# RWKV stage: a group prepared in pairs of token blocks inside the turns, head norms with tokens on partitions

## The chip, the core and the metric

One core of a Trainium2 chip runs the whole program. The metric is device microseconds (us) of one execution; the median of three runs is given, and beside it the time and the span of the one execution that the profiler recorded. Engines: PE (TensorE, with its weight loads as PEld), DVE (VectorE), ACT (ScalarE), POOL (GpSimd), SP (which only issues DMAs). Each takes its instructions in order and waits for the others at semaphores.

## The reference

Two transformer blocks over 1024 tokens of width 1024, batch 1, float32. The first block has an RWKV mixer of 512 channels, 8 heads of 64, scanned forwards and backwards. What the change touches:

```python
w_log = -softplus(-(w0 + tanh(w_lo) @ w_up)) - 0.5      # for each of two directions
decay = exp(-exp(w_log))
a = sigmoid(a0 + a_lo @ a_up)
kk = heads(k * k_k)
kk = kk * rsqrt(maximum(sum(kk * kk, axis=-1), 1e-24))  # norm of a head's 64 channels, per token
k = k * (1.0 + (a - 1.0) * k_a)
b = kk * a
# scan:  sa = S @ -kk_t;  S = S * w_t + sa b_t^T + v_t k_t^T;  y_t = S @ r_t
bonus = sum(r * k * r_k, axis=-1) * v
```

## The kernel before

The stage is `rwkv_mix` (the block at L1127). Channels lie on partitions: `z` holds 16 tiles of 128 channels by 1024 tokens, among them r (0 to 3), k (4 to 7), v (8 to 11), the inner parts of the two decay loras (12) and of the rate lora (rows 0 to 63 of 13). Two *groups* of four heads (two tiles each) are worked one after the other. A group has 8 *turns*; turn j takes token block j of the forward direction and block 7 - j of the backward one together, 128 tokens each, in two chunks of 64. `t = 8 g + j` numbers the 16 turns.

A turn has five levels that build the inverse of a triangular matrix: PE product `mx` (L1512 is the helper of all small products), DVE mask (L1824), PE product `xx`, ACT copy `x` (L1380), DVE transpose (L1835). After them come two steps m = 0 and 1: right side (L1793), `u` (half copied by ACT, L1391, half by DVE, L1845), state update (L1849) and output. Between these, each engine has the *front* of turn t + 1 (scores, masks L1779, transposed keys, `nv` L1348) written into fixed places, and ACT the exponentials of turn t + 2 (L1314, L1320). GpSimd scales the keys (`factors`, `queries`, `ends`) and starts the inverse (`first_inverse`, L1470 and L1474). Where there is no next turn in the group (`ahead` is 0), these places are empty. All this order is written by hand, per engine.

Ahead of a group's turns stands its preparation, for each of its two tiles over all 1024 tokens: PE spreads the inverse norms over 128 rows (L1593) and forms three lora sums (L1601); ACT makes the rate (L1358), the factor of k (L1363) and two sigmoids (L1367); DVE makes kk (L1803), b (L1808) and two cumulated sums by scans (L1810, L1813); GpSimd the new k (L1485). The preparation of group 1 waits for the last state of group 0; after it come the first front and first exponentials with nothing beside them. At the end of a group DVE forms r * k * r_k in place (L1862) and ACT moves y to z (L1406).

At the start of the stage ACT squares k * k_k for four tiles (L1303), PE sums each head into rows 64 to 95 of PSUM (L1580), and DVE and ACT take maximum, root and reciprocal of a 32x1024 tile (L1770, L1305, L1773). The stationary of these sums, `head_rows`, comes with the DMA of the masks.

`Marks` are named semaphore counts: an engine adds one after each named step, and `by(name, t)` is the count that this step of turn t gives.

## Time and profile before

| | us |
|---|---|
| median of 3 runs | 3366.47 |
| lowest, highest | 3364.25, 3366.64 |
| profiled execution, its time | 3372.69 |
| profiled execution, its span (first to last instruction) | 3370.8 |
| RWKV stage in it, first DMA to the last copy of y | 688.3 to 1214.7 |
| busy: PE, PEld, DVE, ACT, POOL | 3012.5, 2455.8, 1636.2, 1059.5, 365.7 |

The profile is of one execution, 6.2 us above the median.
### The profile page before, as it was taken

To read this page: it belongs to the slowest core of one execution; us is meant where nothing else is said; L and a number is where in the kernel's file an instruction comes from. 1 tells how busy PE (TensorE), PEld (TensorE's weight loads), DVE (VectorE), ACT (ScalarE), POOL (GpSimd) and SP (SyncE) were. 2 spreads that over 40 slices of the span, in tenths; PEclk is the share of its full clock that TensorE was granted. 3 is DMA by queue.
4 is the path that set the end of the run, shared out by engine and by line. 5 is a ranking of instruction groups with operands and counts; after the bars stand their busy time and mean duration, and the time that the engine had idled before them with its cause. 6 is when DMAs were issued, how large, how long until landed. Compare 5 with 4: busy or idle time off the path is not lost.

```text
span 3370.8 us, 54412 instructions
## 1 busy us (share of the span) xinstructions
PE 3012.5 (89%) x23584; PEld 2455.8 (73%) x23584; DVE 1636.2 (49%) x2306; ACT 1059.5 (31%) x1496; POOL 365.7 (11%) x380
## 2 busy tenths in 40 slices
PE   6955569958868878999999999999999999999997
PEld 5834457828848846788888888778788788888886
DVE  4848868743444443653424332566544453334323
ACT  3232331122222222433323222553324433233322
POOL 1103322224424410000000000000000000000000
PEclk8975669968969978999999999999999999999998
DMA  3410004200000003222232222222222222223222
GB/s 123 144 38 0 0 6 142 95 29 4 4 2 4 4 28 106 89 93 94 94 100 88 94 97 97 97 85 94 91 97 94 88 94 94 100 95 119 100 94 81
DMA packets 71853, 252.79 MB, mean 75 GB/s; under 512 B 7377, under 2 KB 10321, under 8 KB 71377
## 3 DMA queue, kind: packets, MB, share of 16 engines
q1 hardware_dynamic: 62848, 217.01, 19.2%
q0 software_dynamic: 8784, 32.51, 2.7%
q8 instruction: 180, 2.95, 0.4%
q14 instruction: 41, 0.33, 0.0%
HBM read 245.29 MB, written 4.19 MB: 74 GB/s over the span
## 4 chain that ended last, share of the span: by engine, by line
PE 58%; DVE 2%; ACT 1%; issue 0%; DMA 0%; DVEq 0%; ACTq 0%
PE be_ps L2465 42%; PE be_ps L2486 14%; PE be_ps L2499 1%; DVE be_ring L2255 1%; PE be_ps L2207 0%; PE be_ps L2201 0%; ACT be_whi L2532 0%; DVE be_raw_r L2638 0%; DMA be_raw<-in_w_out 0%; DVE be_total L2220 0%; DVE ext_r L2265 0%; DVE big L2228 0%; ACT big L2538 0%; DVE big L2237 0%; ACT be_ring L2162 0%
## 5 line engine op out<-in xcount | busy, mean ns | idle before, releaser
L2638 DVE TENSOR_TENSOR be_raw_r<-be_raw,be_whi 128x1024 fp32r<-128x1024 f32 x361 | 442.3, 1225 | 991.6 <-ACT be_whi L2532 991.2
L2465 PE MATMUL be_ps<-ext_r,be_whi 128*128 128x512 f32 x2304 | 716.4, 392 | 15.3 <-PEq L1875 8.6
L2532 ACT CAST be_whi<-be_raw 128x1024 fp32r<-128x1024 f32 x361 | 378.9, 1049 | 866.6 <-DMA be_raw<-in_ffn_down 315.8
L2465 PE MATMUL be_ps<-big_r,be_whi 128*128 128x512 f32 x2048 | 641.8, 394 | 2.4 <-DVE big_r L2263 2.4
L2465 PEld LDWEIGHTS be_ps<-ext_r,be_whi 128*128 128x128 f32 x2304 | 433.8, 189 | 108.8 <-issue 10.2
L2465 PEld LDWEIGHTS be_ps<-big_r,be_whi 128*128 128x128 f32 x2048 | 383.2, 188 | 96.8 <-DVE big_r L2263 3.1
L2465 PE MATMUL be_ps<-ext_r,be_raw_r 128*128 128x512 f32 x1152 | 450.2, 391 | 0.0
L2465 PE MATMUL be_ps<-big_r,be_raw_r 128*128 128x512 f32 x1024 | 408.1, 398 | 0.0
L2486 PE MATMUL be_ps<-ext_r,be_whi 128*128 128x512 f32 x1152 | 354.6, 389 | 0.0
L2465 PEld LDWEIGHTS be_ps<-ext_r,be_raw_r 128*128 128x128 f32 x1152 | 217.7, 189 | 45.6
L2486 PEld LDWEIGHTS be_ps<-ext_r,be_whi 128*128 128x128 f32 x1152 | 216.2, 188 | 44.9
L2465 PEld LDWEIGHTS be_ps<-big_r,be_raw_r 128*128 128x128 f32 x1024 | 192.2, 188 | 44.9
L2486 PE MATMUL be_ps<-ext_r,be_raw_r 128*128 128x512 f32 x576 | 224.1, 389 | 0.0
L2486 PEld LDWEIGHTS be_ps<-ext_r,be_raw_r 128*128 128x128 f32 x576 | 108.1, 188 | 22.6
L864 PE MATMUL gm_ps_score<-gm_qk_l 64*128 64x128 f32 x448 | 59.6, 411 | 52.7 <-DVE gm_qk_l L989 52.6
L2443 POOL DMA_DIRECT2D out<-big x1 | 0.9, 852 | 973.5 <-DVE big L2237 973.5
L1512 PE MATMUL rw_ps<-rw_x,rw_by_beta 64*64 64x32 f32 x2560 | 96.1, 227 | 4.7 <-ACT rw_x L1380 2.8
L1512 PEld LDWEIGHTS rw_ps<-rw_x,rw_by_beta 64*64 64x64 f32 x2560 | 88.3, 143 | 11.9 <-ACT rw_x L1380 6.8
L864 PEld LDWEIGHTS gm_ps_score<-gm_qk_l 64*128 64x128 f32 x448 | 46.9, 283 | 66.4 <-DVE gm_qk_l L989 63.7
L2440 POOL DMA_DIRECT2D ext<-in_p x2 | 1.4, 712 | 831.3 <-PE be_ps L2486 831.3
L2566 ACT CAST ext_r<-be_gate 128x512 fp32r<-128x512 f32 x72 | 44.7, 621 | 143.4 <-DVE be_gate L2659 143.4
L2560 ACT ACTIVATE be_gate<-be_ps 128x512 f32<-128x512 f32 x88 | 52.6, 598 | 99.9 <-PE be_ps L2465 99.9
(340 smaller groups left out, 4272.8 us busy)
## 6 DMA issues: line engine op xcount, KB each, us to landing
be_raw<-in_ffn_gate SPq DMA_DIRECT2D x88, 512.0 KB, 3.3
be_raw<-in_ffn_up SPq DMA_DIRECT2D x88, 512.0 KB, 3.3
be_raw<-in_ffn_down SPq DMA_DIRECT2D x88, 512.0 KB, 3.3
be_raw<-in_conv_in SPq DMA_DIRECT2D x48, 512.0 KB, 3.3
gp_ada<-in_ada POOLq DMA_DIRECT2D x24, 512.0 KB, 3.5
rp_ada<-in_ada POOLq DMA_DIRECT2D x24, 512.0 KB, 4.4
be_raw<-in_w_out SPq DMA_DIRECT2D x16, 512.0 KB, 3.4
be_raw<-in_ple_gate SPq DMA_DIRECT2D x16, 512.0 KB, 3.3
```

Of the source, the lines that this page charges most:

```text
L864: mm = pe.matmul(ps_score[:, n % 2, par, i * BLK:(i + 1) * BLK], src[rows, 1, i], src[rows, 0, i], start=True, stop=True)
L1512: return pe.matmul(out, lhs, moving, start=start, stop=True, skip_group_check=True)
L2255: dve.scalar_tensor_tensor(s.ring[:, i % 2], self.h(i), self.gain(i), self.ps[:, 6] if plan.copy is None else s.kept[:, :], ALU.mult, ALU.mult
L2440: pool.dma_start(p_raw[:, :, cols(half)], a["p"][:, :, cols(half)]).then_inc(p_loaded[half], 16)
L2443: pool.dma_start(out[:, :, cols(0)], big[:, 0:KD, cols(0)]).then_inc(stored[0], 16)
L2465: mm = pe.matmul(ps[:, bank], part[:, k * P:(k + 1) * P], xs(k), start=(k == 0 and i == 0), stop=(k == KD - 1 and i == 2))
L2486: mm = pe.matmul(ps[:, m], part[:, m * P:(m + 1) * P], x, start=(j == 0 and i == 0), stop=(j == NF - 1 and i == 2))
L2499: mm = pe.matmul(ps[:, steps.bank[n, g]], part[:, at], x[:, k, cols(half)], start=(k == 0 and i == 0), stop=(k == 1 and i == 2))
L2532: act.copy(w.hi[:, n % 3], w.raw[:, n % 3]).then_inc(w.hi_ready, 1)
L2560: act.activation(s.gate[:, j % 2, 0:HALF], ps[:, steps.bank[n, 0]], ACT.Silu).then_inc(act_took, 1)
L2566: act.copy(inner(f, j)[0], s.gate[:, j % 2, 0:HALF]).then_inc(a_hi_made, 1)
L2638: dve.tensor_tensor(w.lo(n), w.raw[:, n % 3], w.hi[:, n % 3].bitcast(F32), ALU.subtract).then_inc(w.lo_ready, 1)
```

## The change

There is one run of 16 turns instead of two of 8. The preparation of a group is cut into four *pairs* of token blocks (p and 7 - p, 256 tokens, both tiles), which is what turns p and 7 - p need. Pair s = 4 g + p. `due(t)` says which pair is prepared in turn t: that of turn t + 2. So turns 0 and 1 prepare the last two pairs of group 0, turns 6 to 9 the four of group 1; the lora sums of the decay and their sigmoids are made at the end of the turn before (turns 0, 5, 6, 7 and 8). Pairs 0 and 1 stand ahead of turn 0, with the decay part of pair 2. `bonus` and `replace_k` of group 0 run inside turn 8. The lora and spreading products of a turn use the one PSUM bank LT, handed from engine to engine.

The head sums now have tokens on partitions: 8 products per tile, each with the squares of a block as the 128x128 stationary and a constant of 2 columns as the moving operand, into 128x64 in all. The constant is in the part that has been loaded since the beginning. The spreading takes one column of this, broadcast to 64, as the stationary and the identity as the moving operand.

```diff
+    out[:, CONST["eps"], HEAD_COLUMNS:HEAD_COLUMNS + 2] = p // 64 == np.arange(2)[None]
...
-        kk_scale = z[64:96, 13]
+        kk_scale = sb("kk_scale", [P, HEAD_PAIRS, NBLK, 2])
...
+        squares = [x[:, 0].rearrange("p d h q k t -> p (d h q k t)") for x in (by_beta, by_kappa)]
+        rate, k_factor = (z[:, 15, n * HALF:(n + 1) * HALF].rearrange("p (q n t) -> p q n t", q=2, n=2) for n in two)
...
+        AT_START = ((4, 5, 6), (1, 2, 0))
...
+        def pair_bank(bank, q):
+            return ps[:, bank, q * 4 * CH:(q + 1) * 4 * CH].rearrange("p (n t) -> p n t", n=2)
...
+        def in_pair(a, p):
+            return a.rearrange("p (n t) -> p n t", t=BLK)[:, p:NBLK - p:NBLK - 1 - 2 * p]
+        def due(t):
+            g, j = divmod(t + 2, n_turns)
+            return (g, j, n_pairs * g + j) if g < n_groups and j < n_pairs else None
+        def turns(turn):
+            for t in range(n_groups * n_turns):
+                turn(*divmod(t, n_turns), t, t % 2, min(2, n_groups * n_turns - 1 - t))
...
+            def sigmoid_of_sum(d, g, p, s, bank=LT):
+                act.wait_ge(*pe_pair.by(f"lora{d}", s))
+                if g:
+                    act.wait_ge(*act_exp.by("e_beta", g * n_turns - 1))
+                for q in two:
+                    ins = act.activation(in_pair(cum[:, d, q], p), pair_bank(bank, q), ACT.Sigmoid,
+                                         bias=vec(core, "w0", 2 * g + q + 4 * d))
+                ins.then_inc(*act_pair(f"sig{d}"))
+            def rates(g, s, bank=LT):
+                act.wait_ge(*pe_pair.by("lora_rate", s))
+                if s:
+                    act.wait_ge(*dve_pair.by("b", s - 1))
+                    act.wait_ge(*act_pair.by("k_factor", s - 1))
+                for q in two:
+                    ins = act.activation(rate[:, q], pair_bank(bank, q), ACT.Sigmoid, bias=vec(core, "a0", 2 * g + q))
+                ins.then_inc(*act_pair("rate"))
+                act.wait_ge(*act_pair.by("rate", s))
+                if s:
+                    act.wait_ge(*pool_pair.by("k", s - 1))
+                for q in two:
+                    i = 2 * g + q
+                    ins = act.activation(k_factor[:, q], rate[:, q], ACT.Identity, bias=ka_rest[:, i:i + 1],
+                                         scale=vec(core, "k_a", i))
+                ins.then_inc(*act_pair("k_factor"))
+            def exps(t):
+                g, j = divmod(t, n_turns)
+                if j < n_pairs:
+                    act.wait_ge(*dve_pair.by("cum1", n_pairs * g + j))
...
+            for p in two:
+                for d in two:
+                    sigmoid_of_sum(d, 0, p, p, AT_START[p][d])
+                rates(0, p, AT_START[p][2])
+            for d in two:
+                sigmoid_of_sum(d, 0, 2, 2)
+            exps(0)
...
+                    if n == 1 and due(t):
+                        rates(due(t)[0], due(t)[2])
+                    if n == 3 and ahead == 2:
+                        exps(t + 2)
...
+                if g and j == 0:
+                    replace_k(g - 1)
+                if ahead:
+                    v_out(t + 1, 1 - par)
+                for m in two:
+                    act.wait_ge(*pe_made.by(f"u{m}", t))
+                    act.copy(u[chunks[0]].rearrange("p h q t -> p (h q t)"), ps[chunks[0], R0 + 1, P:3 * P]
+                             ).then_inc(*act_made(f"u{m}"))
+                    if m == 0 and ahead:
+                        nv_out(t + 1, dve_made.by("rhs1", t))
+                    if due(t + 1):
...
+                        sigmoid_of_sum(m, *due(t + 1))
...
+            def replace_k(g):
+                act.wait_ge(y_taken, (g + 1) * n_turns)
                 act.wait_ge(*dve_group.by("rk", g))
                 for q in two:
                     act.copy(z[:, 4 + 2 * g + q], y[:, q]).then_inc(k_replaced, 1)
...
+            def new_keys(g, p, s):
+                pool.wait_ge(*act_pair.by("k_factor", s))
+                pool.wait_ge(*dve_pair.by("kk", s))
                 for q in two:
-                    k_i = z[:, 4 + 2 * g + q]
-                    pool.wait_ge(*act_pair.by("k_scale", 2 * g + q))
-                    pool.wait_ge(*dve_pair.by("kk", 2 * g + q))
-                    pool.tensor_tensor(k_i, k_i, tmp, ALU.mult).then_inc(*pool_pair("k"))
-                pool.wait_ge(*pool_pair.by("k", 2 * g + 1))
-                pool.wait_ge(*dve_pair.by("b", 2 * g + 1))
...
+                    k = in_pair(z[:, 4 + 2 * g + q], p)
+                    ins = pool.tensor_tensor(k, k, k_factor[:, q], ALU.mult)
+                ins.then_inc(*pool_pair("k"))
+            for p in two:
+                new_keys(0, p, p)
...
+                if due(t):
+                    new_keys(*due(t))
+                if ahead == 2:
+                    factors(*divmod(t + 2, n_turns), t + 2)
...
+            at = CONST["eps"] * P + HEAD_COLUMNS
+            head_columns = core.const[:, at:at + 2]
             for n in range(HEAD_PAIRS):
                 pe.wait_ge(kk_squared, n + 1)
-                for hf in two:
-                    ins = pe.matmul(ps[64:96, hf], head_rows(core, n), squares[n % 2][:, hf * HALF:(hf + 1) * HALF],
-                                    start=(n == 0), stop=(n == HEAD_PAIRS - 1))
+                for j in range(NBLK):
+                    ins = pe.matmul(ps[:, 0, (n * NBLK + j) * 2:(n * NBLK + j) * 2 + 2],
+                                    squares[n % 2][:, j * BLK:(j + 1) * BLK], head_columns, start=True, stop=True)
                 ins.then_inc(kk_summed, 1)
-            pe.wait_ge(kk_scaled, 2)
-            pe.wait_ge(setup, 2)
+            pe.wait_ge(setup, 1)
             pe.wait_ge(cleared, 2)
...
+            pe.wait_ge(loaded, 16)
+            def lora_sum(name, g, p, s, bank=LT):
+                n, rows, w_n, z_n = {"lora0": (0, slice(0, 64), 0, 12), "lora1": (1, slice(64, 128), 0, 12),
+                                     "lora_rate": (2, slice(0, 64), 1, 13)}[name]
+                pe.wait_ge(lora_loaded, g * 16 + 16)
+                if name == "lora0" and s >= 2:
+                    pe.wait_ge(*dve_pair.by("kk", s - 1))
+                elif bank == LT:
+                    pe.wait_ge(*act_pair.by({"lora1": "sig0", "lora_rate": "sig1"}[name], s))
+                for q in two:
+                    ins = pe.matmul(pair_bank(bank, q), lora[rows, w_n, q], in_pair(z[rows, z_n], p), start=True, stop=True)
+                ins.then_inc(*pe_pair(name))
+            def spread_kk_scale(g, p, s, bank=LT):
+                pe.wait_ge(kk_scaled, 3)
+                if bank == LT:
+                    pe.wait_ge(*act_pair.by("rate", s))
+                for q in two:
+                    for n, j in enumerate((p, NBLK - 1 - p)):
+                        for h in heads:
+                            of_head = kk_scale[:, 2 * g + q, j, h:h + 1].to_broadcast([P, CH])
+                            ins = pe.matmul(pair_bank(bank, q)[rows_of(h), n], of_head, cst(core, "ident"),
+                                            start=True, stop=True)
                 ins.then_inc(*pe_pair("kk_scale"))
...
+            for p in two:
+                for name, bank in zip(("lora0", "lora1", "lora_rate"), AT_START[p]):
+                    lora_sum(name, 0, p, p, bank)
+                if p:
+                    pe.wait_ge(*dve_pair.by("kk", 0))
+                spread_kk_scale(0, p, p, 7)
+            lora_sum("lora0", 0, 2, 2)
+            lora_sum("lora1", 0, 2, 2)
...
+                    if n == 1 and due(t):
+                        lora_sum("lora_rate", *due(t))
+                    if n == 2 and due(t):
+                        spread_kk_scale(*due(t))
...
+                    if due(t + 1) and m == 0:
+                        lora_sum("lora0", *due(t + 1))
+                    if m and ahead:
+                        front_nv(t + 1, 1 - par)
+                    if due(t + 1) and m:
+                        lora_sum("lora1", *due(t + 1))
...
+            per_head = kk_scale.rearrange("p n j h -> p (n j h)")
+            dve.tensor_scalar(per_head, ps[:, 0, 0:HEAD_PAIRS * NBLK * 2], 1e-24, None, ALU.max).then_inc(kk_scaled, 1)
             dve.wait_ge(setup, 2)
-            dve.reciprocal(kk_scale, kk_scale).then_inc(kk_scaled, 1)
+            dve.reciprocal(per_head, per_head).then_inc(kk_scaled, 1)
+            dve.wait_ge(kk_scaled, 2)
+            dve.tensor_scalar(per_head, per_head, -1.0, None, ALU.mult).then_inc(kk_scaled, 1)
+            def cumulated(d, g, p, s):
+                dve.wait_ge(*act_pair.by(f"sig{d}", s))
+                mask = keep[:, 0:BLK] if d == 0 else keep[:, BLK:0:-1]
+                for q in two:
+                    for j in (p, NBLK - 1 - p):
+                        x_block = cum[:, d, q, j * BLK:(j + 1) * BLK]
+                        x_block = x_block if d == 0 else x_block[:, ::-1]
+                        ins = dve.tensor_tensor_scan(x_block, mask, x_block, 0.0, ALU.mult, ALU.add)
+                ins.then_inc(*dve_pair(f"cum{d}"))
+            def removal_keys(g, p, s, bank=LT):
+                dve.wait_ge(*pe_pair.by("kk_scale", s))
+                if g:
+                    dve.wait_ge(*pool_front.by("alpha", g * n_turns - 1))
+                for q in two:
+                    i = 2 * g + q
+                    ins = dve.scalar_tensor_tensor(in_pair(kk[:, q], p), in_pair(z[:, 4 + i], p), vec(core, "k_k", i),
+                                                   pair_bank(bank, q), ALU.mult, ALU.mult)
+                ins.then_inc(*dve_pair("kk"))
+            def removals(g, p, s):
+                dve.wait_ge(*act_pair.by("rate", s))
+                dve.wait_ge(*dve_pair.by("kk", s))
+                if g:
+                    dve.wait_ge(*pool_front.by("beta", g * n_turns - 1))
+                for q in two:
+                    ins = dve.scalar_tensor_tensor(in_pair(b[:, q], p), in_pair(kk[:, q], p), -1.0, rate[:, q],
+                                                   ALU.mult, ALU.mult)
+                ins.then_inc(*dve_pair("b"))
...
+            def bonus(g):
+                dve.wait_ge(*pool_front.by("rho", (g + 1) * n_turns - 1))
...
+                    if due(t) and n in (1, 2):
+                        cumulated(n - 1, *due(t))
+                    if due(t) and n == 3:
+                        removal_keys(*due(t))
+                    if due(t) and n == 4:
+                        removals(*due(t))
+                    if g and j == 0 and n == 4:
+                        bonus(g - 1)
...
+                if j == n_turns - 1 and g + 1 < n_groups:
+                    empty_state(g + 1)
+            turns(turn)
+            bonus(n_groups - 1)
```

Three places show how the order moves. First ACT, the end of turn 6 (`rw_u` is the half of u, twice; `rw_x` begins the next turn). Before:

```order
L1341 COPY rw_v_tok<-rw_ps 128x2x4x64
L1391 COPY rw_u<-rw_ps 64x256
L1348 COPY rw_nv<-rw_ps 128x512
L1391 COPY rw_u<-rw_ps 64x256
L1380 COPY rw_x<-rw_ps 128x2x64x2
```

Of the change:

```order
L1386 COPY rw_v_tok<-rw_ps 128x2x4x64
L1426 COPY rw_u<-rw_ps 64x256
L1393 COPY rw_nv<-rw_ps 128x512
L1328 ACT_TABLE_LOAD
L1328 ACTIVATE rw_cum<-rw_ps,vec 128x2x128 x2
L1426 COPY rw_u<-rw_ps 64x256
L1328 ACTIVATE rw_cum<-rw_ps,vec 128x2x128 x2
L1411 COPY rw_x<-rw_ps 128x2x64x2
```

A table load and two sigmoids stand ahead of the second copy of u.

Then DVE, levels 1 to 4 of turn 1 (the masks of the products are `rw_mx`; `rw_by_beta` and `rw_by_kappa` are those of the front). Before:

```order
L1835 STREAM_TRANSPOSE rw_xt<-rw_x 128x512
L1824 TENSOR_TENSOR rw_mx<-rw_ps,rw_masks 128x2x32x4
L1779 TENSOR_TENSOR rw_by_beta<-rw_ps,rw_masks 128x512
L1835 STREAM_TRANSPOSE rw_xt<-rw_x 128x512
L1779 TENSOR_TENSOR rw_by_beta<-rw_ps,rw_masks 128x512
L1824 TENSOR_TENSOR rw_mx<-rw_ps,rw_masks 128x2x16x8
L1779 TENSOR_TENSOR rw_by_kappa<-rw_ps,rw_masks 128x512
L1835 STREAM_TRANSPOSE rw_xt<-rw_x 128x512
L1779 TENSOR_TENSOR rw_by_kappa<-rw_ps,rw_masks 128x512
L1824 TENSOR_TENSOR rw_mx<-rw_ps,rw_masks 128x2x8x16
```

Of the change:

```order
L1930 STREAM_TRANSPOSE rw_xt<-rw_x 128x512
L1848 SCALAR_TENSOR_TENSOR rw_cum<-rw_masks,rw_cum 128x128 x4
L1919 TENSOR_TENSOR rw_mx<-rw_ps,rw_masks 128x2x32x4
L1875 TENSOR_TENSOR rw_by_beta<-rw_ps,rw_masks 128x512
L1930 STREAM_TRANSPOSE rw_xt<-rw_x 128x512
L1875 TENSOR_TENSOR rw_by_beta<-rw_ps,rw_masks 128x512
L1848 SCALAR_TENSOR_TENSOR rw_cum<-rw_masks,rw_cum 128x128 x4
L1919 TENSOR_TENSOR rw_mx<-rw_ps,rw_masks 128x2x16x8
L1875 TENSOR_TENSOR rw_by_kappa<-rw_ps,rw_masks 128x512
L1930 STREAM_TRANSPOSE rw_xt<-rw_x 128x512
L1875 TENSOR_TENSOR rw_by_kappa<-rw_ps,rw_masks 128x512
L1857 SCALAR_TENSOR_TENSOR rw_kk<-big,vec,rw_ps 128x256 x2
```

Scans (`rw_cum`) and the removal keys (`rw_kk`) stand ahead of the masks of the following products.

Last PE, the second step of turn 7 of the kernel before, from its last products to the first of the next group:

```order
L1512 MATMUL rw_ps<-rw_u,rw_beta_tok 64x64 x8
L1512 MATMUL rw_ps<-rw_by_beta,rw_u 64x64 x8
L1593 MATMUL rw_ps<-big,rw_masks 128x512 x2
L1601 MATMUL rw_ps<-big,rw_lora 128x512 x6
L1593 MATMUL rw_ps<-big,rw_masks 128x512 x2
L1601 MATMUL rw_ps<-big,rw_lora 128x512 x6
L1512 MATMUL rw_ps<-rw_queried,rw_beta 64x128 x16
```

Of the change, the same place in turn 7, with the front of turn 8 (`rw_v_tok`) and a lora sum, and then the first product of turn 8:

```order
L1559 MATMUL rw_ps<-rw_v_tok,rw_by_kappa 64x64 x16
L1645 MATMUL rw_ps<-big,rw_lora 128x256 x2
L1559 MATMUL rw_ps<-rw_by_kappa,rw_v_tok 64x64 x8
L1559 MATMUL rw_ps<-rw_u,rw_beta_tok 64x64 x8
L1559 MATMUL rw_ps<-rw_by_beta,rw_u 64x64 x8
L1559 MATMUL rw_ps<-rw_x,rw_by_beta 64x32 x16
```

The wide products between the groups are gone, and a lora sum stands between the front and the output product.

## Rows read from the trace of the kernel before

**Rows 1.** The page, part 1: busy us, share of the span, instructions.
```profile
PE 3012.5 (89%) x23584; PEld 2455.8 (73%) x23584; DVE 1636.2 (49%) x2306; ACT 1059.5 (31%) x1496; POOL 365.7 (11%) x380
```

**Rows 2.** Table by stretches; busy PE, PEld, DVE, ACT, POOL, then PE's clock.
```profile
690.00:762.00 72.00, 36.58 (x218) 15.94 (x220) 28.59 (x16) 23.95 (x32) 24.57 (x28) 0.59 0.08 31
...
950.00:1030.00 80.00, 53.53 (x964) 39.72 (x962) 34.80 (x40) 24.08 (x43) 29.56 (x32) 0.64 0.01 2
```

**Rows 3.** Timeline, second state updates: start us, length, engine, line; brackets: idle before.
```profile
793.00 0.42 DVE L1849 TENSOR_TENSOR rw_state<-rw_ps,rw_state_kept 128x256 f32<-128x256 f32 x1 [3.06 <-PE rw_ps L1512]
...
911.55 0.42 DVE L1849 TENSOR_TENSOR rw_state<-rw_ps,rw_state_kept 128x256 f32<-128x256 f32 x1 [2.44 <-PE rw_ps L1512]
...
937.81 0.42 DVE L1849 TENSOR_TENSOR rw_state<-rw_ps,rw_state_kept 128x256 f32<-128x256 f32 x1 [1.93 <-PE rw_ps L1512]
...
1039.62 0.42 DVE L1849 TENSOR_TENSOR rw_state<-rw_ps,rw_state_kept 128x256 f32<-128x256 f32 x1 [1.94 <-PE rw_ps L1512]
```

**Rows 4.** Timeline of the stage's start.
```profile
695.40 3.62 PE L1580 MATMUL rw_ps<-rw_by_beta,rw_masks 128*32 128x512 f32 x4 [12.38 <-DMA rw_masks<-in_const]
...
707.06 6.54 DVE L1773 RECIPROCAL big<-big 32x1024 f32<-32x1024 f32 x1 [1.12 <-ACT big L1305]
...
741.37 0.70 ACT L1320 ACTIVATE rw_e_beta<-rw_cum 128x256 f32<-128x256 f32 x2
```

**Rows 5.** Timeline, PE: wide products at either clock, whole weights, half weights.
```profile
713.66 3.78 PE L1593 MATMUL rw_ps<-big,rw_masks 32*128 32x512 f32 x4 [9.05 <-DVE big L1773]
...
976.94 1.98 PE L1593 MATMUL rw_ps<-big,rw_masks 32*128 32x512 f32 x4
...
503.50 3.74 PE L1041 MATMUL gf_rs<-const,gf_root 128*128 128x128 f32 x32
...
478.74 1.13 PE L894 MATMUL gm_ps_k<-gm_v_tok,gm_k_tok 128*64 128x128 f32 x8
```

**Rows 6.** Timeline, the wide preparation: GpSimd's k beside DVE's scans.
```profile
732.99 3.38 POOL L1485 TENSOR_TENSOR big<-big,rw_by_kappa 128x1024 f32<-128x1024 f32 x1 [5.65 <-DVE rw_kk L1803]
734.10 4.43 DVE L1810 TENSOR_TENSOR_SCAN rw_cum<-rw_masks,rw_cum 128x1024 f32<-128x1024 f32 x1
...
738.45 2.26 DVE L1813 TENSOR_TENSOR_SCAN rw_cum<-rw_masks,rw_cum 128x1024 f32<-128x1024 f32 x1
...
724.99 2.35 POOL L1485 TENSOR_TENSOR big<-big,rw_by_kappa 128x1024 f32<-128x1024 f32 x1 [26.75 <-ACT rw_by_kappa L1363]
```

**Rows 7.** Timeline: a table load, and the end of a turn on ACT and PE.
```profile
721.23 1.28 ACT L1358 ACT_TABLE_LOAD   x1 [14.20 <-PE rw_ps L1601]
...
722.52 1.11 ACT L1358 ACTIVATE rw_by_beta<-rw_ps,vec 128x1024 f32<-128x1024 f32 x1
...
886.33 0.58 ACT L1348 COPY rw_nv<-rw_ps 128x512 f32<-128x512 f32 x1 [4.11 <-PE rw_ps L1512]
...
886.82 0.36 ACT L1391 COPY rw_u<-rw_ps 64x256 f32<-64x256 f32 x1
...
887.23 0.46 PE L1512 MATMUL rw_ps<-rw_u,rw_beta_tok 64*64 64x64 f32 x16 [0.71 <-ACT rw_u L1391]
```

**Rows 8.** Timeline, DVE: level 2 of turn 4, and the bonus at the seam.
```profile
871.61 0.65 DVE L1779 TENSOR_TENSOR rw_by_beta<-rw_ps,rw_masks 128x512 f32<-128x512 f32 x1
872.18 0.41 DVE L1824 TENSOR_TENSOR rw_mx<-rw_ps,rw_masks 128x256 f32<-128x256 f32 x1
...
966.37 2.48 DVE L1862 SCALAR_TENSOR_TENSOR big<-big,vec 128x1024 f32<-128x1024 f32 x2
```

**Rows 9.** Table by stretches of 4 us in turn 6 (columns as in Rows 2).
```profile
924.00:928.00 4.00, 2.98 (x119) 2.77 (x117) 1.50 (x3) 1.35 (x4) 0.00 (x0) 1.00 0.02 4
928.00:932.00 4.00, 3.34 (x87) 2.99 (x86) 1.11 (x3) 0.66 (x2) 0.00 (x0) 0.56 0.00 0
```

**Rows 10.** Timeline, PE: the same product at either clock in turn 7.
```profile
941.01 1.12 PE L1512 MATMUL rw_ps<-rw_x,rw_by_beta 64*64 64x32 f32 x32
...
948.29 1.92 PE L1512 MATMUL rw_ps<-rw_x,rw_by_beta 64*64 64x32 f32 x32 [0.47 <-ACT rw_x L1380]
```

516 lines of the change are left out of this document (219 added, 297 removed).

## The prediction

> **What bounds the kernel now.** Begin with the page: TensorE is busy for 89% of the span [rows 1], so DVE, ACT and GpSimd matter only where TensorE waits for them. The RWKV stage lies at 688 to 1214 us. The table by stretches [rows 2] says where that stage loses time. In the 72 us at its start TensorE works for 36.6 us, and in the 80 us around the seam between the groups for 53.5, at mean clocks of 0.59 and 0.64. Next the ends of the turns, which are the second state update of each (DVE, L1849) [rows 3]. From turn 0 to turn 6 six turns take 937.81 - 793.00 = 144.8 us, 24.1 each. I call this an ordinary turn. From the end of turn 6 to the end of turn 8, also two turns, it is 1039.62 - 937.81 = 101.8 us. The reader should see the seam as one number: 53.5 us more than two ordinary turns. It holds the last turn, whose TensorE has no work for a next one and falls to the low clock, and then a preparation in which everything waits. Last, the timeline inside the stage: within a turn the engines alternate, TensorE product, DVE mask, TensorE product, ACT copy, with gaps of half a microsecond. That matters most for the price of what is added: an engine that is busy for half of a turn is not free at the place where new work is put.
>
> **What the change removes.** *The seam.* Turn 7 now carries the front of turn 8, and turn 8 follows as turn 1 follows turn 0. The two turns cost 48.3 us before any added work: a gain of **53.5 us**. The bounds are narrow: without the one turn of 26.3 us the mean is (144.8 - 26.3) / 5 = 23.7, and the gain 54.4.
>
> *The start.* Before, the constants land first (TensorE waits until 695.40), then come the head sums, one reciprocal of 6.54 us on a 32x1024 tile, two serial pairs of wide operations, and the first exponentials end at 742.07 (the second e_beta of the row at 741.37, 0.70 long) [rows 4]. Now the sums wait only for the first square, at 692.0. They are 32 products of a 128x128 weight with 2 columns, 64 records. A weight of that size with 128 columns passes in 3.74 / 32 = 0.117 us at the high clock [rows 5]; at the low clock twice that. Bounds 7.5 and 15 us; I take low for the first two head pairs' share and high after it, ending at about 702. Four tiny operations on 128x64 follow (the reciprocal by the row 6.54 / 16 = 0.41 us), about 1.4 us with their waits. Then the pairs: a lora sum of a pair is two products of 256 columns, four records; four records of 512 columns take 1.98 us at the high clock and 3.78 at the low one [rows 5], so half-width ones take 0.86 or 1.7. On DVE a pair costs eight scans of 128 columns (2.26 us for 1024 columns [rows 6], so 0.28 and some start each, 0.37; 3.0 in all) and four operations of some 0.4 (256 columns take 0.42 in the state rows [rows 3]): 4.6 us. Two pairs one after the other from about 704.5 end near 714 to 715 with the waits on GpSimd; then the third pair's lora sums and sigmoids (each waits for the other, some 5 us), a table load of 1.28 and the exponentials of turn 0: they end at about 722 or 723. Gain **19 us**; at the low clock throughout (15 us for the sums, twice 0.86 for each lora sum) it is 11, at the high clock 23. From the first exponentials to the first product of turn 0 nothing changes.
>
> **What it adds.** Group 1's four pairs go into turns 6 to 9, and group 0's last two into turns 0 and 1: six turns with a *middle* part, and five turn *ends* (0, 5, 6, 7, 8) with the lora sums of the following turn's pair. Nothing of this is free merely because its engine has idle time.
>
> *An end.* ACT must copy nv, then load the sigmoid table (the turn's exponentials displaced it), then take two sigmoids of 128x256, and only then copies its half of u for step 1. Before, u follows nv at once: 886.33 and 886.82, and the product with u starts at 887.23 [rows 7]. The load is 1.28 us, the next activation starting 0.01 after it (721.23 + 1.28 and 722.52); the sigmoids about 0.9 (1.11 for 1024 columns, a fixed share remaining). So u comes 2.2 us late. But TensorE is in order: `lora1` stands ahead of its output product and waits for the first sigmoid, so 0.86 of lora sum and 0.5 of output product follow the sigmoid instead of filling the gap. From 886.9 + 0.2 (lora0 put ahead) + 1.28 + 0.9 + 0.86 + 0.5, the product with u starts at about 890.7: **3.5 us** late. The low bound is 2.2, if TensorE's part overlaps. Five ends: **17.5 us** (11 to 20).
>
> *A middle.* Level 1: lora_rate is 0.86 us of TensorE ahead of the second product; the four scans of direction 0 (1.4 us) run under it: 1.0. Level 2: the spreading products are 16 records of 64-column weights; eight such records took 1.13 us at the low clock [rows 5], which is half of the 0.23 each that whole weights take there, so 16 take about 0.94 at the high clock. The four scans of direction 1 stand between a mask of `by_beta` and the mask of the third product, and there DVE has no gap: the row at 871.61 ends when the one at 872.18 begins [rows 8]. 0.94 + 1.4, less some slack, is 2.1. Level 3: two `kk` operations in the same kind of place, 0.8 to 0.9. Level 4: two `b` operations, of which 0.5 lies in a gap: 0.2. Together 4.2. ACT's share (a second table load and 2 us of rates) fits, since it waits about 3 us between copies. To this comes GpSimd. In the wide preparation a scan took 4.43 us instead of 2.26 while GpSimd's product of `k` (3.38 instead of 2.35) ran beside it [rows 6]: they do not run together. The scans of direction 1 start in the same instant as GpSimd's two 1.3 us operations of `first_inverse`. Bounds 0 and 2.5 us; I take 0.9, since DVE is first in the queue but not in all four scans. **5.1 us** a middle, six of them: **31 us** (25 to 40).
>
> *The bonus.* `bonus(0)`, two operations, 2.48 us [rows 8], moves from the seam into level 4 of turn 8, ahead of a mask on the chain, beside GpSimd's factors: 2.5 to 5.3, taken as **4**. The copy of y into z (2 us of ACT) lies under it.
>
> *The clock.* Ordinary turns live near the edge: after 4 us with TensorE busy for 2.98 the granted clock was 0.56 in the next four [rows 9], and that turn took 26.3 us (911.55 to 937.81) [rows 3], 2.3 over an ordinary one. Every end now holds 3 us of waiting. I charge 1.5 us for each of five, **7.5** (0 to 15).
>
> The semaphores, masks and the extra sixteen or so waits are under these. DMA: the lora weights of group 1 are asked for after turn 1 and have four turns to land.
>
> The sum: 53.5 + 19 - 17.5 - 31 - 4 - 7.5 = 12.5, so **13 us** gained. The profiled execution has a span of 3370.8 and took 3372.69, 6.2 above the median of the runs, 3366.47; the gain is taken from the median: **3353 us**.
>
> **A rule against the row.** The trace shows a table load of 1.28 us and no gap behind it [rows 7]. The Trainium skill, ScalarE: Activation LUTs, section What ACT_TABLE_LOAD costs, says that a switch also pays a drain of about 1.38 us, 2.66 together. By that rule the five loads on the path would cost 6.9 us more, an estimate from that page, and the sum would be 6. The rows of this case do not bear it out, so it is a rival only.
>
> **Rivals.** *Hidden after all*: only TensorE's own records count, 1.8 a middle and 1.1 an end: 73 - 10.8 - 5.5 = 57 gained, 3310 us. For it: DVE 49%, ACT 31% busy. Against it: [rows 8], no gap at the place. Chance 0.13. *Low clock in the loaded turns*, the one that ends slower: the waits at the ends and behind the scans take TensorE down for whole turns. A product of 32 records takes 1.12 us high and 1.92 low [rows 10], ten of them 8 us a turn, and the front and state products about half as much again: 12 us a turn. Five turns less the 7.5 charged is 52 us, so 39 lost, 3405 us; it decides from two and a quarter such turns (13 gained and 7.5 charged against 2 x 12). More likely three or four of them than five: 3380 to 3400. The clock row [rows 9] speaks for it, the bigger share of lora and spreading records against it. Chance 0.18. *The lock in full*: each middle pays 2.5 instead of 0.9, 9.6 more: 3363 us. Chance 0.12. *The start gains little*: sums and loras at the low clock, 11 instead of 19: 3361 us. Chance 0.10. *Each table load waits longer on ACT than its row says*, 1.38 more at five ends, as a pipeline that must run empty first: 3360 us. Chance 0.07.
>
> **How the numbers follow.** The forecast has 0.40, its own range 3340 to 3362. The range from 3325 to 3384 takes in the three middle rivals and the near half of the slow one; outside lie most of the hidden case and the far part of the slow one, 0.2. About 0.2% (6.7 us) is what a measurement can tell from no change. Faster: 0.36 of the forecast, 0.13, and 0.13 of the 0.29 in the three rivals near 3361: 0.62. Same: the rest of these, 0.20. Slower: 0.18.
>
> **What the new profile would show.** The step from the end of turn 6 to that of turn 8 falls from 101.8 to about 72 (48, two middles, two ends, the bonus, two clock charges); if it is near 50, the work is hidden. First e_beta ends 34 us after the stage begins instead of 54. In an end, ACT shows nv, load, sigmoid, u, and TensorE's product with u starts 3.5 us later. A scan pair under `first_inverse` shows longer scans than those of direction 0. Turns 10 to 14 stay at 24 each. What would make it wrong: scans much longer than 0.37, or a clock below 0.8 through turns 6 to 9.

## The result, and the profile after the change

The changed kernel takes 3397.16 us (median of 4 runs, 3389.85 to 3403.86), the kernel before it 3365.36 us (4 runs, 3363.84 to 3366.64, three of them those of the table ahead of the prediction). The ratio is 1.0094, with a 95% interval of 1.0070 to 1.0118: **the change makes the kernel 32 us slower**. The forecast of 3353 us and its range up to 3384 both missed, and the sign was wrong. The profiled execution has a span of 3388.1 us and took 3389.85, so it is the fastest of the four. That of the kernel before took 3372.69, 6.2 above its median. The two traces are therefore only 17 us apart, where the medians are 32.

The page, part 1, as in [rows 1]:

```profile
PE 3050.3 (90%) x23792; PEld 2511.7 (74%) x23792; DVE 1644.2 (49%) x2387; ACT 1082.4 (32%) x1554; POOL 367.1 (11%) x392
```

The share of TensorE's busy time went up, from 89% to 90%. That says nothing good: a product at the low clock is busy for longer. The start times of the second state updates (DVE, now L1952) tell more. Two of the sixteen, the ends of turns 7 and 8, as in [rows 3]; the idle time in brackets, 6.55 and 7.01 us, was 1.9 to 3.1 in the rows of before:

```profile
1006.66 0.42 DVE L1952 TENSOR_TENSOR rw_state<-rw_ps,rw_state_kept 128x256 f32<-128x256 f32 x1 [6.55 <-PE rw_ps L1559]
...
1050.07 0.42 DVE L1952 TENSOR_TENSOR rw_state<-rw_ps,rw_state_kept 128x256 f32<-128x256 f32 x1 [7.01 <-PE rw_ps L1559]
```

From all of them, read in the same way, come the lengths of the turns. "Stage to end 0" runs from the first operation of the stage on DVE to the end of turn 0; a turn n runs from the end of turn n - 1 to its own. The middle parts are in turns 0, 1 and 6 to 9, the lora sums in the ends of turns 0 and 5 to 8.

| us | before | changed |
|---|---|---|
| stage to end 0 | 104.3 | 100.6 |
| turn 1 | 23.7 | 35.6 |
| turns 2, 3, 4 | 24.3, 23.6, 23.2 | 23.9, 23.5, 23.2 |
| turn 5 | 23.8 | 27.0 |
| turn 6 | 26.3 | 41.0 |
| turn 7 | 27.5 | 41.0 |
| turn 8 | 74.3 | 43.4 |
| turn 9 | 24.8 | 36.1 |
| turns 10 to 15 together | 144.7 | 144.5 |
| whole stage, to end 15 | 520.4 | 539.6 |

The seam is gone, as it should be: turns 7 and 8 took 101.8 us and take 84.4. But turns 6 and 9, which had nothing to win, and turn 1 lose 14.7, 11.3 and 11.9 us.

Where the time goes in a loaded turn stands in the table by stretches, through turn 6 (925.2 to 966.1 us) and most of turn 7 (columns: busy PE, PEld, DVE, ACT, POOL, then PE's clock, DMA share, GB/s):

```profile
936.00:940.00 4.00, 1.03 (x20) 1.04 (x22) 3.51 (x5) 0.00 (x0) 1.92 (x2) 0.74 0.02 4
940.00:944.00 4.00, 4.00 (x96) 4.00 (x95) 2.49 (x5) 3.04 (x8) 0.46 (x1) 0.50 0.00 0
...
960.00:964.00 4.00, 1.47 (x4) 1.16 (x4) 0.00 (x0) 2.60 (x5) 2.74 (x4) 0.72 0.00 0
964.00:968.00 4.00, 4.00 (x104) 3.50 (x106) 1.43 (x4) 0.84 (x2) 0.62 (x1) 0.50 0.02 4
...
976.00:980.00 4.00, 1.03 (x31) 0.77 (x30) 4.00 (x7) 0.00 (x0) 2.57 (x2) 0.86 0.00 0
980.00:1000.00 20.00, 19.84 (x423) 18.50 (x425) 7.37 (x16) 5.67 (x13) 5.74 (x9) 0.52 0.02 4
```

In 936 to 940 TensorE works for 1.03 of 4 us. From then on the granted clock is 0.50, half speed, although TensorE is busy for nearly all of the next twelve. In 960 to 964 it starves again (1.47 of 4), in 976 to 980 once more, and each time the low clock follows, for one stretch of 4 us behind the second gap and for most of the 20 us behind the third. The two places in a turn are always the same. The first is level 2, shown here in turn 0, on the timeline (start, length, engine, line; in brackets the idle time before and what ended it):

```profile
755.67 1.33 DVE L1848 TENSOR_TENSOR_SCAN rw_cum<-rw_masks,rw_cum 128x128 f32<-128x128 f32 x4
...
761.12 3.41 DVE L1848 TENSOR_TENSOR_SCAN rw_cum<-rw_masks,rw_cum 128x128 f32<-128x128 f32 x4
...
761.29 1.31 POOL L1514 TENSOR_TENSOR rw_by_beta<-rw_by_beta,rw_masks 128x512 f32<-128x512 f32 x1 [9.65 <-DVE rw_by_beta L1875]
762.67 1.26 POOL L1518 TENSOR_TENSOR rw_xt<-rw_by_beta,rw_masks 128x512 f32<-128x512 f32 x1
764.46 0.39 DVE L1919 TENSOR_TENSOR rw_mx<-rw_ps,rw_masks 128x256 f32<-128x256 f32 x1
...
764.90 1.81 PE L1559 MATMUL rw_ps<-rw_mx,rw_xt 64*64 64x32 f32 x29 [2.97 <-DVE rw_mx L1919]
```

The four scans of direction 0 take 1.33 us. The same four of direction 1 take 3.41, because GpSimd's two operations of `first_inverse` (1.31 and 1.26) lie inside them, and TensorE stands still for 2.97 us until the mask behind them is done.

The second place is the end of a turn, here turn 6 (ACT copies nv, loads a table, takes the sigmoid, copies u; TensorE's `lora1` stands ahead of the product with u):

```profile
955.47 0.42 DVE L1952 TENSOR_TENSOR rw_state<-rw_ps,rw_state_kept 128x256 f32<-128x256 f32 x1 [2.23 <-PE rw_ps L1559]
...
959.65 0.58 ACT L1393 COPY rw_nv<-rw_ps 128x512 f32<-128x512 f32 x1 [6.47 <-PE rw_ps L1559]
960.26 1.28 ACT L1328 ACT_TABLE_LOAD   x1
...
961.55 0.84 ACT L1328 ACTIVATE rw_cum<-rw_ps,vec 128x256 f32<-128x256 f32 x2
...
962.28 0.35 ACT L1426 COPY rw_u<-rw_ps 64x256 f32<-64x256 f32 x1
...
962.53 2.04 PE L1645 MATMUL rw_ps<-big,rw_lora 64*128 64x256 f32 x4 [2.92 <-ACT rw_cum L1328]
...
964.99 0.65 PE L1559 MATMUL rw_ps<-rw_u,rw_beta_tok 64*64 64x64 f32 x16
...
965.70 0.42 DVE L1952 TENSOR_TENSOR rw_state<-rw_ps,rw_state_kept 128x256 f32<-128x256 f32 x1 [6.55 <-PE rw_ps L1559]
```

TensorE waits 2.92 us for the sigmoid, then `lora1` takes 2.04 us at the low clock. From the first state update of the turn to the second, 955.47 to 965.70, it is 10.2 us, against 4.8 in an ordinary turn.

Last, the start of the stage, as in [rows 4]:

```profile
694.28 3.58 PE L1628 MATMUL rw_ps<-const,rw_by_beta 128*128 128x2 f32 x16 [9.02 <-ACT rw_by_beta L1317]
...
708.02 3.78 PE L1645 MATMUL rw_ps<-big,rw_lora 64*128 64x256 f32 x12
...
729.05 0.70 ACT L1365 ACTIVATE rw_e_beta<-rw_cum 128x256 f32<-128x256 f32 x2
...
700.00:708.00 8.00, 8.00 (x38) 8.00 (x38) 0.00 (x0) 2.43 (x2) 0.58 (x2) 0.50 0.00 0
```

The head sums run at 3.4 us for each head pair, where the forecast had the later two at the high clock (16 records of 0.117, 1.9 us), with the clock at 0.50 and TensorE busy for 8.00 of 8 us. The first e_beta ends at 729.75, which is 39.2 us after the stage's block begins at 690.5, against 53.8 before. That is 14.6 us gained instead of 19.

### The profile page after: what moved, and what is told of

Read it like the earlier page. It is cut to its first block, busy times and chain, and to the rows that moved or that the text cites. A ratio compares the mean times of both kernels' runs of the same rounds, so it can differ in the third digit from the quotient of the medians.

```text
span 3388.1 us, 55041 instructions
## 1 busy us (share of the span) xinstructions
PE 3050.3 (90%) x23792; PEld 2511.7 (74%) x23792; DVE 1644.2 (49%) x2387; ACT 1082.4 (32%) x1554; POOL 367.1 (11%) x392
## 3 DMA queue, kind: packets, MB, share of 16 engines
q8 instruction: 182, 2.98, 0.4%
## 4 chain that ended last, share of the span: by engine, by line
PE 57%; DVE 2%; ACT 1%; DMA 0%; issue 0%; DVEq 0%; ACTq 0%
PE be_ps L2566 42%; PE be_ps L2587 14%; DVE be_ring L2356 1%; PE be_ps L2600 1%; PE be_ps L2308 0%; PE be_ps L2302 0%; ACT be_whi L2633 0%; DVE be_raw_r L2739 0%; DMA be_raw<-in_w_out 0%; DMA be_raw<-in_ple_gate 0%; DVE be_total L2321 0%; DVE ext_r L2366 0%; ACT big L2639 0%; DVE big L2329 0%; DVE big L2338 0%
## 5 line engine op out<-in xcount | busy, mean ns | idle before, releaser
L2566 PEld LDWEIGHTS be_ps<-ext_r,be_whi 128*128 128x128 f32 x2304 | 432.5, 188 | 108.2 <-issue 10.2
L1559 PE MATMUL rw_ps<-rw_x,rw_by_beta 64*64 64x32 f32 x2560 | 105.3, 238 | 1.9 <-ACT rw_x L1411 1.4
L1559 PEld LDWEIGHTS rw_ps<-rw_x,rw_by_beta 64*64 64x64 f32 x2560 | 99.8, 158 | 6.8 <-ACT rw_x L1411 4.0
L1559 PE MATMUL rw_ps<-rw_mx,rw_xt 64*64 64x32 f32 x2048 | 83.4, 236 | 19.4 <-DVE rw_mx L1919 18.4
L1559 PEld LDWEIGHTS rw_ps<-rw_mx,rw_xt 64*64 64x64 f32 x2048 | 78.7, 156 | 26.1 <-DVE rw_mx L1919 26.1
```

The source lines that it names most:

```text
L1559: return pe.matmul(out, lhs, moving, start=start, stop=True, skip_group_check=True)
L2566: mm = pe.matmul(ps[:, bank], part[:, k * P:(k + 1) * P], xs(k), start=(k == 0 and i == 0), stop=(k == KD - 1 and i == 2))
```

## The experiments

The theory, called A in what follows: each stall of about 3 us takes TensorE's clock to half for up to half a turn, and that, more than the added work and the stalls themselves, is the loss. Its rival B: the stalls and the added instructions cost their own length and no more. The runs were made in three sessions, in each of which the kernel before ran too (medians of 3369.23, 3367.13 and 3363.88 us), but the changed kernel did not. So a difference from its 3397.16 can be off by some 4 us; the ratio to before, given with each run, is the safer number.

### The scans freed from GpSimd, and the ends rearranged

The first edit, on GpSimd alone:

```diff
+                if due(t):
+                    pool.wait_ge(*dve_pair.by("cum1", due(t)[2]))
                 if ahead:
                     first_inverse(t + 1, 1 - par)
```

> Only GpSimd's first_inverse of a turn with a middle waits until the scans of direction 1 are done. In the changed kernel those four scans took 3.41 us instead of 1.33, and TensorE stood still for 2.97 us. Theory A (each stall of about 3 us takes the clock to 0.50 for half a turn, and the low clock is most of the loss): scans at 1.33, a gap of about 1 us, turns 1 and 9 fall from 36 to about 29 us, turns 0, 6, 7, 8 by about 5 each, since their other stall stays; median about 3363 us (3355 to 3372). Theory B (the waits alone, clock beside the point): 2.1 us in each of six middles, 12.6 in all, 3384 us. Theory C (the lock moves to the masks of level 3): scans at 1.33 but no gain, 3397 us.

Measured: 3362.81 us (10 runs, 3355.28 to 3382.75), 0.9989 of before (0.9973 to 1.0005). Turn 1, the next level 2 of that kernel:

```profile
794.60 1.36 DVE L1850 TENSOR_TENSOR_SCAN rw_cum<-rw_masks,rw_cum 128x128 f32<-128x128 f32 x4
...
796.04 1.27 POOL L1514 TENSOR_TENSOR rw_by_beta<-rw_by_beta,rw_masks 128x512 f32<-128x512 f32 x1 [10.93 <-DVE rw_cum L1850]
796.19 0.68 DVE L1877 TENSOR_TENSOR rw_by_kappa<-rw_ps,rw_masks 128x512 f32<-128x512 f32 x1
...
796.33 1.06 PE L1561 MATMUL rw_ps<-rw_mx,rw_xt 64*64 64x32 f32 x30 [0.92 <-DVE rw_mx L1921]
```

The scans are back at 1.36 us and TensorE waits 0.92 instead of 2.97. Turn 1 falls from 35.6 to 28.1 us, turn 9 from 36.1 to 32.8, turns 6, 7 and 8 by 8.8, 4.1 and 4.5. The stall that was removed is 2.1 us long, the turns fall by up to four times that, and the whole by 34 us, where B said 12.6. Turn 9 did not come down to the 29 us that A gave it. C is out as well: the stall does not move to the masks of level 3. The row of the mask into by_kappa shows it: it has one input in PSUM and one in SBUF, runs beside GpSimd's operation, and takes 0.68 us as always.

The second edit puts ACT's first sigmoids behind both copies of u, and `lora1` with its sigmoids into level 1 of the next turn:

```diff
                     if m == 0 and ahead:
                         nv_out(t + 1, dve_made.by("rhs1", t))
-                    if due(t + 1):
-                        sigmoid_of_sum(m, *due(t + 1))
+                if due(t + 1):
+                    sigmoid_of_sum(0, *due(t + 1))
...
             def turn(g, j, t, par, ahead):
+                if t and due(t):
+                    sigmoid_of_sum(1, *due(t))
...
                         from_state(t, par, 0)
+                        if t and due(t):
+                            lora_sum("lora1", *due(t))
...
-                    if due(t + 1) and m:
-                        lora_sum("lora1", *due(t + 1))
```

> Only the ends are rearranged: ACT copies nv and both halves of u before it loads the table and takes the first sigmoids, and lora1 with its sigmoids goes into level 1 of the next turn. The products with u no longer wait for a load or a sigmoid. Theory A: the stall of about 3 us at five ends goes, turn 5 falls from 27.0 to 24, turns 6, 7, 8 from 41-43 to the 36 us of turns 1 and 9, which have no such end: about 25 us in all, 3372 us (3365 to 3378). Theory B (waits alone): 3.5 us at five ends, 17.5 in all, and lora1 costs 0.9 where it stands now: 3384 us.

Measured: 3359.37 us (10 runs, 3350.68 to 3365.41), 0.9972 of before (0.9962 to 0.9981). Turn 5, which has only an end, falls from 27.0 to 23.6, as A and B both said (3.4 us). Turns 6, 7 and 8 fall from 41.0, 41.0 and 43.4 to 33.1, 30.5 and 37.4. Both theories said too little here: the gain is 38 us in all, 13 more than A and 20 more than B expected. Perhaps a turn with one stall instead of two comes back to the high clock for longer than A assumed; in this run turns 7 and 8 together have a clock of 0.87, where the changed kernel has 0.66.

> Both edits together. Theory A: no stall of 3 us is left, the granted clock stays near 1.00 through turns 1 and 5 to 9, each turn with a middle takes 24 + 4 to 5 us instead of 36 to 43: about 70 to 75 us less than the changed kernel, 3323 us (3315 to 3335), which is more than the two edits give one by one. Theory B (waits alone): the two gains add, 12.6 + 13, 3371 us.

Measured: 3329.04 us (4 runs, 3328.01 to 3333.49), 0.9888 of before (0.9871 to 0.9904). That is inside A's range and 42 us below B's number. One part of the expectation was wrong: 68 us is about the sum of the two single gains, 34 and 38, not more. Turns 6, 7 and 9 take 28.2, 28.2 and 27.8 us. Turns 7 and 8 in the table, from the end of turn 6 to the end of turn 8, first in the changed kernel, then in this one:

```profile
966.12:1050.49 84.37, 70.56 (x1532) 63.53 (x1532) 38.57 (x74) 26.17 (x54) 27.15 (x32) 0.66 0.01 2
```

```profile
928.97:991.64 62.67, 53.96 (x1535) 46.70 (x1532) 34.02 (x74) 26.03 (x55) 26.89 (x33) 0.92 0.01 3
```

The granted clock is 0.66 against 0.92, with the same work to do (1532 and 1535 of TensorE's records). In turn 7 alone it is 1.00 in this kernel, in turn 8 it is 0.85.

### The stalls left in place, and filled

This run separates clock and waits. Nothing is rearranged; in each of the two gaps TensorE gets five products that nobody needs.

```diff
+            def filler():
+                for _ in range(5):
+                    mm(ps[:, Y0, 2 * P:4 * P], cst(core, "ident"), core.const[:, 0:2 * P], start=False)
...
                     elif ahead and n == 3:
                         front_kappa(t + 1, 1 - par, 0)
+                        if due(t):
+                            filler()
...
                     if due(t + 1) and m:
+                        filler()
                         lora_sum("lora1", *due(t + 1))
```

> The changed kernel with its waits as they are, and five products of a 128x128 weight with 256 columns (about 2.2 us of TensorE at the high clock) put into each of the two stalls of a loaded turn, into columns that nobody reads. Theory A: the clock stays up although everything waits as long as before: turns 6 to 8 fall from 41-43 to about 34, turns 1 and 9 from 36 to 31, 3359 us (3350 to 3370). Theory B: nothing is gained, 3397 us or more, up to 2 us for each filler that is longer than its gap.

Measured: 3350.9 us (4 runs, 3346.27 to 3352.2), 0.9944 of before (0.9927 to 0.996). Work was added, nothing that the chain waits for was moved, and the kernel became **46 us faster** than the changed one (50 by the two ratios to before). Level 2 of turn 7, and turns 7 and 8 in the table:

```profile
953.24 3.42 DVE L1855 TENSOR_TENSOR_SCAN rw_cum<-rw_masks,rw_cum 128x128 f32<-128x128 f32 x4
...
957.03 1.06 PE L1559 MATMUL rw_ps<-rw_mx,rw_xt 64*64 64x32 f32 x29 [0.62 <-DVE rw_mx L1926]
```

```profile
944.40:1014.84 70.44, 62.31 (x1575) 53.04 (x1573) 38.14 (x73) 26.18 (x55) 27.18 (x32) 0.95 0.01 3
```

The scans are as long as ever (3.42 us), but TensorE stands idle for only 0.62 us of the gap instead of 2.97, and its clock is 0.95 in turns 7 and 8 together, and 1.00 in turns 1, 5, 6, 7 and 9. Turns 6 and 7 take 32.3 us each instead of 41.0, turn 8 38.1 instead of 43.4, turns 1 and 9 28.8 and 28.7 instead of 35.6 and 36.1, and the stage 495.9 instead of 539.6. B is out. The run also gives the waits without the clock: turn 1, with a middle only, is 5.6 us above that kernel's ordinary 23.2; turn 5, with an end only, 3.6 above.

### One such stall, in the kernel before

The kernel before the change, with nothing of the change in it, and four extra scans of constants in turns 2 and 11:

```diff
                         if ahead and n in (2, 3):
                             front_out(t + 1, 1 - par, ("beta1", "kappa1")[n - 2])
+                        if n == 2 and t in (2, 11):
+                            for k in range(4):
+                                dve.tensor_tensor_scan(idle[:, k * BLK:(k + 1) * BLK], keep[:, 0:BLK], keep[:, 0:BLK],
+                                                       0.0, ALU.mult, ALU.add)
```

> The kernel before the change, with nothing of the change in it: in turns 2 and 11 alone DVE does four extra scans of 128 columns (of constants, into columns that nobody reads) at the place where the changed kernel has those of direction 1, behind the mask by_beta of level 2 and beside GpSimd's first_inverse. Each of the two turns had 24.3 and 24.4 us. Theory A (a stall costs its length and then the low clock): the scans take about 3.4 us, TensorE stands still about 3 us, the granted clock is at 0.50 behind it and each turn gets 6 to 10 us longer, 30 to 34 us. Theory B (only its length): 26.5 to 27.5 us. The median of the whole moves by 12 to 20 us by A, by 5 to 6 by B.

Measured: 3376.93 us (7 runs, 3367.11 to 3384.16), 1.0036 of before (1.0021 to 1.0052). Turn 2, timeline and table:

```profile
818.37 3.40 DVE L1844 TENSOR_TENSOR_SCAN big<-rw_masks 128x128 f32<-128x128 f32 x4
...
822.14 1.57 PE L1513 MATMUL rw_ps<-rw_mx,rw_xt 64*64 64x32 f32 x29 [2.97 <-DVE rw_mx L1825]
...
820.00:824.00 4.00, 1.86 (x42) 1.86 (x46) 2.68 (x5) 0.13 (x1) 1.18 (x1) 0.81 0.00 0
824.00:828.00 4.00, 4.00 (x96) 4.00 (x90) 1.71 (x3) 2.30 (x8) 2.31 (x4) 0.50 0.02 4
```

The scans and the stall repeat what the changed kernel shows (3.40 us for 3.41, and 2.97 for 2.97). Turns 2 and 11 take 28.6 and 29.8 us, where that execution's ordinary turn is 23.2: 5.4 and 6.6 us for a stall of 2.97. Against the same two turns of the kernel before (24.3 and 24.4) it is 4.3 and 5.4. So a single stall costs one and a half times to twice its length. A's lower end of 30 us was too high, B's 27.5 too low; the median moved by 13 us, which is inside A's 12 to 20. The two traces do not show it over the whole stage (520.0 us here, 520.4 before): this profiled execution is 6.5 us below its median and that of before 6.2 above, and other turns, turn 6 above all (23.6 for 26.3), are shorter here. This run is the weakest of those that speak for A; e4_filler is the strongest.

### The bonus

In the kernel with both edits turn 8 still takes 34.5 us, 6.3 more than turn 7. Its level 4 on DVE and TensorE, and the clock behind it:

```profile
976.11 2.94 DVE L1912 SCALAR_TENSOR_TENSOR big<-big,vec 128x1024 f32<-128x1024 f32 x2
978.98 0.41 DVE L1923 TENSOR_TENSOR rw_mx<-rw_ps,rw_masks 128x256 f32<-128x256 f32 x1
...
979.44 1.80 PE L1563 MATMUL rw_ps<-rw_xt,rw_mx 64*64 64x32 f32 x29 [2.97 <-DVE rw_mx L1923]
...
980.00:984.00 4.00, 3.95 (x61) 3.46 (x60) 0.86 (x3) 1.99 (x4) 1.14 (x2) 0.50 0.02 4
```

The two operations of `bonus(0)` take 2.94 us beside GpSimd, TensorE waits 2.97, and the clock is 0.50 behind it: a third stall with the same sequel. The edit:

```diff
-                    if g and j == 0 and n == 4:
-                        bonus(g - 1)
+                if j == n_turns - 1 and g + 1 < n_groups:
+                    bonus(g, 0)
                 for m in two:
...
                                     ).then_inc(*dve_made(f"u{m}"))
+                    if m == 0 and j == n_turns - 1 and g + 1 < n_groups:
+                        bonus(g, 1)
                     dve.wait_ge(*pe_made.by(f"end{m}", t))
```

> The kernel with both edits (e3_both), and the two operations of bonus(0) taken out of level 4 of turn 8 and put, one by one, into gaps of DVE at the end of turn 7 (behind the last transposed block, and behind the copy of u of step 0). In e3_both turn 8 takes 34.5 us, the other loaded turns 28.2. Theory: the bonus on the chain beside GpSimd's factors costs 6.3 us, turn 8 falls to 28 to 29, turn 7 grows by 0 to 1: 3323 to 3324 us. Rival: what is long in turn 8 is the copy of y into z on ACT and the first turn of a group as such: turn 8 stays above 33 us, 3329.

Measured: 3320.25 us (4 runs, 3315.79 to 3324.6), 0.9859 of before (0.9838 to 0.988). DVE in level 5 and the end of turn 7:

```profile
949.07 1.53 DVE L1911 SCALAR_TENSOR_TENSOR big<-big,vec 128x1024 f32<-128x1024 f32 x1
...
951.08 1.28 DVE L1911 SCALAR_TENSOR_TENSOR big<-big,vec 128x1024 f32<-128x1024 f32 x1
```

Turn 8 falls to 28.9 us. Turns 6 and 7 read 29.2 instead of 28.2 in this execution; turn 6 holds nothing of the edit, so of its growth I can say no more than that such differences of a microsecond come and go. The rival, that turn 8 is long as the first turn of a group, is out.

### Level 4 instead of level 2

This kernel has the ends of e2_ends. The scans of direction 1 go to level 4, behind the mask and ahead of a transpose that has to wait for ACT anyway, and ACT's exponentials one level later. GpSimd gets no wait.

```diff
                     elif ahead and n == 5:
                         front_x(t + 1)
+                    if due(t) and n == 4:
+                        cumulated(1, *due(t))
...
-                    if due(t) and n in (1, 2):
-                        cumulated(n - 1, *due(t))
+                    if due(t) and n == 1:
+                        cumulated(0, *due(t))
...
-                    if n == 3 and ahead == 2:
+                    if n == (4 if due(t) else 3) and ahead == 2:
                         exps(t + 2)
```

> The ends of e2_ends, and instead of letting GpSimd wait, the four scans of direction 1 stand in level 4 between a mask and the transpose that waits for ACT's copy, where DVE is idle for about 1.5 us; the exponentials go one level later. Theory (a price is set by the gap at the place, not by the length of the work): a middle costs 3.5 to 4 us instead of 4.9, turn 1 takes 26.5 to 27.2, turns 6 and 7 27 instead of 28.2: 3322 to 3325 us. Rival: the factors on GpSimd come too late for kept, or the longer chain at level 4 stalls TensorE: turns of 30 us and more, 3340 us or above.

Measured: 3343.86 us (4 runs, 3343.78 to 3344.9), 0.993 of before (0.9912 to 0.9948): the rival's number. The rival had named a stall of TensorE by the longer chain at level 4 as one of two reasons; the stall is there, but it comes through ACT. Turn 1:

```profile
797.73 1.53 POOL L1531 TENSOR_TENSOR big<-big 128x256 f32<-128x256 f32 x2 [1.74 <-DVE rw_kk L1860]
797.84 2.33 DVE L1851 TENSOR_TENSOR_SCAN rw_cum<-rw_masks,rw_cum 128x128 f32<-128x128 f32 x4
...
799.53 1.28 ACT L1360 ACT_TABLE_LOAD   x1
...
802.26 0.57 ACT L1382 COPY rw_kappa_tok<-rw_ps 128x512 f32<-128x512 f32 x1
...
802.88 0.69 PE L1562 MATMUL rw_ps<-rw_masks,big 64*64 64x64 f32 x32 [2.19 <-ACT rw_kappa_tok L1382]
```

The table load and the exponentials stand ahead of ACT's copy of kappa_tok, and TensorE's next products wait 2.19 us for that copy. The scans, now beside GpSimd's product of the new keys, take 2.33 us. Turn 1 takes 30.7 us instead of 27.8. The next run puts the exponentials behind that copy, lets the new keys wait for the scans, and moves the bonus as above.

```diff
                         kappa_out(t + 1, 1 - par)
+                    if n == 4 and due(t):
+                        exps(t + 2)
...
             def new_keys(g, p, s):
                 pool.wait_ge(*act_pair.by("k_factor", s))
+                pool.wait_ge(*dve_cum.by("cum1", s))
                 pool.wait_ge(*dve_pair.by("kk", s))
```

> In e7_gap_scans TensorE stood still for 2.2 us in front of the value transposes, until ACT's kappa_tok copy, which stood behind the table load and the exponentials, and the scans took 2.33 us beside GpSimd's product of the new keys. Here the exponentials come after the kappa_tok copy, the new keys wait for the scans, and the bonus is placed as in e6_bonus. Theory: no stall is left in a middle, the clock stays up, turn 1 takes 26 to 27.5 us (27.8 in e3_both) and the loaded turns 27 to 28.5: 3312 to 3320 us, at or below e6_bonus (3320). Rival: level 4 has no more room on DVE than level 2 (kk, mask, scans and b all stand there): turns of 29 us and more, 3325 us or above.

Measured: 3317.61 us (4 runs, 3315.73 to 3318.01), 0.9861 of before (0.9844 to 0.9877). In turn 1 the copy now comes ahead of the load, and the scans have their own length:

```profile
790.48 1.36 DVE L1854 TENSOR_TENSOR_SCAN rw_cum<-rw_masks,rw_cum 128x128 f32<-128x128 f32 x4
...
792.31 0.59 ACT L1382 COPY rw_kappa_tok<-rw_ps 128x512 f32<-128x512 f32 x1 [0.15 <-PE rw_ps L1565]
```

Turn 1 takes 27.2 us, turns 6 to 9 27.6, 28.8, 28.7 and 27.3. So the work of a middle costs 4 us in the best place that I found, and the kernel stands at 3318 to 3320 us in either form, 46 to 47 us ahead of the kernel before in the same session, and 77 to 80 ahead of the changed one. Between this one and e6_bonus the intervals do not tell.

### The clock in the head sums

The kernel with both edits, with fourteen products ahead of the head sums:

```diff
             head_columns = core.const[:, at:at + 2]
+            for _ in range(14):
+                pe.matmul(ps[:, LT, 0:2 * P], cst(core, "ident"), core.const[:, 0:2 * P], start=True, stop=True)
```

> The kernel with both edits (e3_both, 3329 us), and ahead of the head sums fourteen products of a 128x128 weight with 256 columns into a bank that is overwritten later: about 6 us at the high clock, in the 8 us in which TensorE has nothing to do at the start of the stage. In the kernels so far the sums ran at 3.4 us for each head pair with the granted clock at 0.50 although TensorE was busy all the time. Theory S1 (the clock was low only because TensorE came out of a pause): it stays at 1.00 through the sums, 1.7 us for each pair unless the squares are late, the sums end 5 to 6 us earlier: 3323 us. Theory S2 (a stream of products of 2 columns does not keep the high clock): it falls back to 0.50 within the sums, the gain is 0 to 2 us: 3328 us.

Measured: 3333.04 us (4 runs, 3329.64 to 3339.19), 0.9903 of before (0.9883 to 0.9923): nothing gained, and from the stage's first operation to the end of turn 0 it is 93.2 us instead of 88.1. TensorE at the start, and the table by stretches:

```profile
689.08 8.18 PE L1630 MATMUL rw_ps<-const 128*128 128x256 f32 x28 [5.80 <-PEq L281]
697.10 1.84 PE L1634 MATMUL rw_ps<-const,rw_by_beta 128*128 128x2 f32 x16
698.80 2.69 PE L1634 MATMUL rw_ps<-const,rw_by_kappa 128*128 128x2 f32 x16
701.35 3.55 PE L1634 MATMUL rw_ps<-const,rw_by_beta 128*128 128x2 f32 x16
...
696.00:700.00 4.00, 4.00 (x32) 3.85 (x30) 0.00 (x0) 1.02 (x1) 2.83 (x5) 0.97 0.01 4
700.00:704.00 4.00, 4.00 (x20) 4.00 (x20) 0.00 (x0) 2.56 (x3) 0.00 (x0) 0.50 0.00 0
```

The added products ran at the low clock for their first part (8.18 us in place of 6), and the sums began 8.0 us after the stage's first operation instead of 3.2. The first head pair's sums then took 1.7 us, at the high clock, as S1 says; in 700 to 704 the clock is at 0.50 again although TensorE had not paused since 689. S2's course came true, but not its number: the added products cost more than they gave. Why the clock falls in this stream, the rows do not tell.

## Why the prediction was wrong

**The sum, term by term.** In the changed kernel's own runs:

- *The seam, 53.5*: right. In e6_bonus, with the bonus off the chain, turns 7 and 8 take 58.0 us. Less two middles of 4.75 (its turns 1 and 9 take 27.8 and 28.1, over 23.2) it is 48.5, and before they took 101.8: 53.3 us.
- *The start, 19*: 14.6. The mis-sized term is above all the head sums: 13.8 us instead of 10, since the clock did not rise in them as I took it to. The bound (15 us) held it. The readings of [rows 5] came out low too: half of 1.98 is 0.99 and not 0.86, and a lora sum measures 1.10 us at the high clock (e4_filler) and 2.04 at the low one; and 1.13 / 8 is 0.14 and not half of 0.23, so 16 spreading records are 1.13 at the high clock and not 0.94 (they measure 1.09).
- *The ends, 3.5 each*: right while the clock is high (1.00 there): turn 5 of e4_filler, with an end only, is 26.8 us, 3.6 over 23.2. At the low clock an end costs 5.4 (10.2 less 4.8 from one state update to the next), and from ACT's copy of nv to the product with u it is 5.3 us in place of 0.9, 4.4 more.
- *The middles, 5.1 each*: 5.6 in e4_filler's turn 1. In it the lock (DVE and GpSimd keeping each other waiting) was under-priced: the scans of direction 1 grow by 2.1 us (3.41 for 1.33), where I took 0.9 of a range to 2.5.
- *The bonus, 4*: 6.3, above its upper bound of 5.3, since it too sets off the low clock.
- *The clock, 7.5*: **44 to 50 us**. It is the difference between the changed kernel and e4_filler, 43.7 in the stage's traces, 46 in the medians and 50 by the ratios, although the filler adds some 2.4 us of work to each gap.

With the measured sizes the sum is 53.5 + 14.6 - 5 x 3.5 - 6 x 5.6 - 6.3 - 45 = -34, and the measurement is -32. That they agree so well is in part luck: in the two traces from which most of the sizes were read, the stage is only 19 us longer. About 7 us of the difference lie in turns 1 to 6 and 9 of the kernel before, which were in all 7.3 us above seven turns of 23.2; the rest was not followed up.

**The step that failed** is the sentence "I charge 1.5 us for each of five". I had the row that priced it: in [rows 9], after one stretch with 2.98 of 4 us busy, the clock was at 0.56 in the next, and the turn was 2.3 longer (26.3 less 24.1 is rather 2.2). From that I took a price for a mild gap and put it on ends in which, by my own working, TensorE would wait 3 us. And I charged the ends alone, not the middles, although the paragraph above had just shown that a mask waits behind scans there. The working on level 2 summed up what DVE has to do and never turned the same numbers round to ask how long TensorE would have nothing. It would have: 1.4 us of scans, plus up to 2.5 of lock, is a gap of up to 3.9 us in each of six turns, and 2.97 was measured. What the runs showed in its place: the gaps behind the scans and those at the ends together cost 44 to 50 us in clock alone, not 7.5, and the turns that have only a middle pay for it too (6.8 and 7.4 us in turns 1 and 9).

**The rival that came true** is the low clock in the loaded turns. Its price of 12 us for each low turn was too high, as no turn is low all the way: the clock costs 8.7 us in turns 6 and 7, 5.3 in turn 8, 6.8 and 7.4 in turns 1 and 9, 5.4 in turn 0 (changed kernel less e4_filler). But six turns have it and not five. What I set against it, the bigger share of lora and spreading records, was wrong: in the table above TensorE is busy for 19.84 of 20 us behind the gap of 976 to 980, with such records among them, and the clock there is 0.52. The chance of 0.18 should have been the largest. Its count of turns was loose too: 13 gained and 7.5 charged are used up by 1.7 turns of 12 us, not by two and a quarter. The rival of the lock in full came true beside it (2.1 of 2.5 us). *Hidden after all* is out. *The start gains little* is half true. *Each table load waits longer* is out: the load at 960.26 takes 1.28 us and the sigmoid begins at 961.55, and the stage's other loads read the same. The Trainium skill, ScalarE: Activation LUTs, section What ACT_TABLE_LOAD costs, gives 2.66 us with a drain; by these rows there is no such drain here.

**The list of what the profile would show.** Turn 6 to turn 8: 84.4, not 72. First e_beta: 39.2 us after the stage begins, not 34. The order nv, load, sigmoid, u in an end: as said. Longer scans under `first_inverse`: as said. Turns 10 to 14: 23.2 to 23.7, as said. "A clock below 0.8 through turns 6 to 9" stood under what would make it wrong, and is what happened (0.67 in turn 6, 0.66 in turns 7 and 8, 0.67 in turn 9). So did the scans much longer than 0.37, 0.85 each in direction 1.

## What to carry to other kernels

Where a tightly wound chain feeds TensorE, ask of every piece of work that is put into it how long TensorE then has nothing to do, and not only how long the piece is: here one gap of 3 us made its turn 4 to 7 us longer, and the changed kernel's gaps cost 44 to 50 us in clock on top of their own length. Two cheap remedies worked: order the small work so that nothing on the chain stands behind it on its engine (the copies of u ahead of the table load, GpSimd behind DVE's scans), or, where a gap must stay, fill it with products whose result is thrown away. The filler is also the quickest test of whether a loss is waiting or clock.

## What the runs showed that I had not expected

- Five useless products in a gap of 3 us, at two places in a turn, made the kernel 46 us faster.
- TensorE at the start of the stage was busy for 8.00 of 8 us in the head sums and its clock stayed at 0.50; brought up ahead of them it fell back within them. I had thought that being busy was enough. What does hold the clock in such a stream was not tried.
- Beside GpSimd some kinds of DVE instruction grew and others did not. Four scans went from 1.33 to 3.41 us beside 2.57 us of GpSimd's work, and the bonus operations (both inputs in SBUF too) took 2.94 instead of the 2.48 of [rows 8]; the masks that read PSUM, 0.69 us, did not grow. The Trainium skill, SBUF — State Buffer, section Who interferes with whom, says that a DVE instruction with two inputs in SBUF contends with a GpSimd instruction that reads SBUF; these rows agree.
- What stays open: the stage's other part of the start. From the first e_beta to the first product of turn 0 it is still 21 us, as it was before, in e3_both at a clock of 0.50 all the way, and no run was made on it.
